# Two gate rows from rounded part and remainder, and eight modulation sums moved

## The reference, cut to what matters

```
mod = silu(c) @ w_ada + b_ada                       # 6 x 2048 values, the same for all tokens
sh1, sc1, g1, sh2, sc2, g2 = split(mod, 6)
h = rms_norm(x, norm1_w) * (1 + sc1) + sh1
... projections of h, two attentions, merged ...
x = x + g1 * (merged @ w_out)
h2 = rms_norm(x, norm2_w) * (1 + sc2) + sh2
x = x + g2 * ((silu(h2 @ w_ffn_gate) * (h2 @ w_ffn_up)) @ w_ffn_down)
return rms_norm(x, final_w)
```

## Time and profile before

| | |
|---|---|
| median of three runs | 2207.69 us |
| the profiled execution, its span from the first to the last instruction | 2206.6 us |
| TensorE busy | 2185.9 us (99%) |
| VectorE busy | 1492.7 us (68%) |
| ScalarE busy | 1013.1 us (46%) |
| GpSimd busy | 266.0 us (12%) |
| moved from HBM | 500.72 MB, 227 GB/s over the span |
| modulation sums on VectorE | 384 |
| loads of `ada_raw`, median to landing | 4.7 us |

### The profile page before, as it was taken

The page is one execution under the profiler, slowest core; times in us unless marked ns, Lnnn a source line. Parts: engine busy times, 40 slices in busy tenths (PEclk is TensorE's granted clock), DMA queues, the critical chain, the costliest instruction groups (busy, mean ns, idle before and its releaser), DMA issues.

```text
span 2206.6 us, 32483 instructions
## 1 busy us (share of the span) xinstructions
PE 2185.9 (99%) x10910; PEld 1849.9 (84%) x10910; DVE 1492.7 (68%) x1995; ACT 1013.1 (46%) x1246; POOL 266.0 (12%) x499
## 2 busy tenths in 40 slices
PE   9999999999999999999999999999999999999998
PEld 8898889988878887898888888888888888888886
DVE  5766668877777878587776768775566655444544
ACT  5445545444444445444555444454444444443433
POOL 2101110112210010701111211110000100000000
PEclk9999999999999999999999999999999999999999
DMA  8867576778986594968666877756776776565564
GB/s 294 246 194 233 177 271 232 194 247 292 304 282 182 164 313 141 262 201 263 220 193 198 294 262 244 250 199 225 237 233 218 255 239 210 176 224 181 186 200 138
DMA packets 200428, 500.72 MB, mean 227 GB/s; under 512 B 31816, under 2 KB 59112, under 8 KB 200048
## 3 DMA queue, kind: packets, MB, share of 16 engines
q1 hardware_dynamic: 166256, 394.10, 55.4%
q0 software_dynamic: 33760, 104.41, 14.9%
q10 hardware_dynamic: 288, 0.52, 0.1%
HBM read 496.84 MB, written 2.15 MB: 226 GB/s over the span
## 4 chain that ended last, share of the span: by engine, by line
PE 90%; DMA 4%; DVE 3%; ACT 1%; issue 1%; POOLq 0%; DVEq 0%; SPq 0%; ACTq 0%
PE ps L2251 73%; PE ps L2295 10%; DMA ada_raw<-in_w_ada_dram 2%; DMA raw<-in_ml_w_in_dram 1%; DVE lo L1225 1%; PE ps L2348 1%; PE ps L2719 1%; PE ps L2708 1%; DVE acc_s L1237 0%; PE ps L2609 0%; PE ps L2791 0%; DVE acc_g L1237 0%; PE ps L2443 0%; PE ps L2444 0%; PE ps L2466 0%
## 5 line engine op out<-in xcount | busy, mean ns | idle before, releaser
L1225 DVE TENSOR_TENSOR lo<-raw,hi 128x1024 fp32r<-128x1024 f32 x731 | 889.7, 1223 | 550.1 <-ACT hi L667 547.6
L667 ACT CAST hi<-raw 128x1024 fp32r<-128x1024 f32 x731 | 763.7, 1052 | 964.4 <-PE ps L2251 742.7
L2251 PE MATMUL ps<-hi,XH 128*128 128x512 f32 x1944 | 609.3, 393 | 3.6 <-DVE lo L1225 1.4
L2251 PE MATMUL ps<-lo,XH 128*128 128x512 f32 x1944 | 602.6, 390 | 0.0
L2251 PE MATMUL ps<-hi,XL 128*128 128x512 f32 x1944 | 602.0, 390 | 0.0
L2251 PEld LDWEIGHTS ps<-hi,XL 128*128 128x128 f32 x1944 | 365.0, 188 | 76.7
L2251 PEld LDWEIGHTS ps<-lo,XH 128*128 128x128 f32 x1944 | 365.0, 188 | 76.5
L2251 PEld LDWEIGHTS ps<-hi,XH 128*128 128x128 f32 x1944 | 360.8, 188 | 78.2 <-issue 4.1
L585 POOL DMA_DIRECT2D ada_raw<-in_w_ada_dram x384 | 206.5, 539 | 1552.2 <-DVE acc_s L1237 895.2
L1237 DVE SCALAR_TENSOR_TENSOR acc_s<-ada_raw,c_act,acc_s 128x512 f32<-128x512 f32 x256 | 191.1, 747 | 20.9 <-DMA ada_raw<-in_w_ada_dram 19.6
L2295 PE MATMUL ps<-XH,hi 128*128 (+1 forms) x504 | 142.9, 284 | 0.0
(11 more groups left out here) (385 smaller groups left out, 1833.1 us busy)
## 6 DMA issues: line engine op xcount, KB each, us to landing
ada_raw<-in_w_ada_dram POOLq DMA_DIRECT2D x384, 256.0 KB, 4.7
raw<-in_w_in_dram SPq DMA_DIRECT2D x136, 512.0 KB, 4.4
raw<-in_ml_w_in_dram SPq DMA_DIRECT2D x128, 512.0 KB, 4.7
raw<-in_w_gate_dram SPq DMA_DIRECT2D x176, 256.0 KB, 2.9
raw<-in_w_up_dram SPq DMA_DIRECT2D x176, 256.0 KB, 3.7
raw<-in_w_down_dram SPq DMA_DIRECT2D x88, 512.0 KB, 4.0
raw<-in_mla_w_in_dram SPq DMA_DIRECT2D x47, 512.0 KB, 4.9
raw<-in_mla_w_out_dram SPq DMA_DIRECT2D x32, 512.0 KB, 4.5
```

Of the source, the lines that this page charges most:

```text
L667: nc.scalar.copy(hi[:, j, :], raw[:, j, :]).then_inc(hi_ready, 1)
L1225: nc.vector.tensor_tensor(lo[:, j, :], raw[:, j, :], hi[:, j, :].bitcast(F32), ALU.subtract) \
L2251: ins = mm(ps[:, o:o + HALF], x, w[:, b % RING, c0:c0 + HALF], start=first, stop=(k == n_rows - 1 and x is xl), skip_group_check=True)
```

## The change

Gate rows: ScalarE rounds the sum `acc_g` into `gate1_hi` or `gate2_hi` (fp32r), in two halves; VectorE writes the remainder `gate_lo` over `acc_g` itself; TensorE adds both parts, with `ones` read as fp32r: eight fp32r matmuls of 128x512 per row in place of eight passes of f32. The roundings and subtractions stand after `kva` for `g1` and, for `g2`, in the second to last FFN pass behind its rounded product. `gate1_hi` lies where `g_row` will be written, `gate2_hi` where `g2_row` will be (over `ada_raw`, whose last sum is then used).

Sums: `z1` has 20 and not 16, `mv1` 17 and not 20, `mo_0` 17 and not 20, `mo_1` 18 and not 20, `mz0` and `mz1` 8 each and not 6. The total is the same, and the sums of `kv` to `mo1`, `mlk` and `mv0` are as many as before but four further on.

Further, the events `z0_half`, `mo1_half` and so on become one counter `first_half`, and `mo1_three` and `down1_three` one counter `three_quarters`; each wait asks for its place in the order in which they are raised.

```diff
-ADA_BESIDE = {"z1": 16, "kv": 12, "z0": 16, "mo0": 16, "mo1": 14, "mlq": 0, "mlk": 4, "mv0": 16, "mv1": 20, "mo_0": 20,
-              "mo_1": 20, "mz0": 6, "mz1": 6, "lo0": 8, "lo1": 10,
+ADA_BESIDE = {"z1": 20, "kv": 12, "z0": 16, "mo0": 16, "mo1": 14, "mlq": 0, "mlk": 4, "mv0": 16, "mv1": 17, "mo_0": 17,
+              "mo_1": 18, "mz0": 8, "mz1": 8, "lo0": 8, "lo1": 10,
...
+        gate1_hi = at("gate1_hi", 136, [P, D], F32R)
+        gate_lo = at("gate_lo", 104, [P, D], F32R)
...
+        gate2_hi = at("gate2_hi", 96, [P, D], F32R)
...
+        def half_of(name):
+
+            return ev("first_half"), HALVES.index(name) + 1
...
+            def gate_hi(dst, units):
+
+                act.wait_ge(ada_used, 16 * units)
+                for q in range(2):
+                    cols_ = slice(q * COLS, (q + 1) * COLS)
+                    nc.scalar.copy(dst[:, cols_], acc_g[:, cols_]).then_inc(ev("gate_hi"), 1)
...
             rest(B_KVA, 8)
+            gate_hi(gate1_hi, 12)
             first4(B_QB)
...
                 ffn_hi(p)
+                if p == FFN_PASSES - 2:
+                    gate_hi(gate2_hi, 24)
...
+            def gate_split(src, n):
+
+                for q in range(2):
+                    cols_ = slice(q * COLS, (q + 1) * COLS)
+                    dve.wait_ge(ev("gate_hi"), 2 * n - 1 + q)
+                    nc.vector.tensor_tensor(gate_lo[:, cols_], acc_g[:, cols_], src[:, cols_].bitcast(F32),
+                                            ALU.subtract).then_inc(ev("gate_lo"), 1)
...
             rest(B_KVA, 8, "kva")
+            gate_split(gate1_hi, 1)
             first4(B_QB)
...
                 ffn_lo(p)
+                if p == FFN_PASSES - 2:
+                    gate_split(gate2_hi, 2)
...
-            def ada_row(name, units):
+            def ada_row(name, src, count):
 
                 g = start(name)
-                pe.wait_ge(ada_used, 16 * units)
+                pe.wait_ge(ev("gate_lo"), count)
                 for n in range(4):
-                    ins = mm(ps[:, g + n * HALF:g + (n + 1) * HALF], ones[:, :], acc_g[:, n * HALF:(n + 1) * HALF],
-                             start=True, stop=True, skip_group_check=True)
+                    for part in (src, gate_lo):
+                        ins = mm(ps[:, g + n * HALF:g + (n + 1) * HALF], ones[:, :].bitcast(F32R),
+                                 part[:, n * HALF:(n + 1) * HALF], start=part is src, stop=part is gate_lo,
+                                 skip_group_check=True)
                 done(ins)
```

More of the change, by code:

```diff
@@ L352, in col, with three_of @@
             return pk[:, o:o + 1]
+        HALVES = ("z0", "mo1", "lo1", "ga0", "ga1", "ob1", "wo1", "down1")
+        THREES = ("mo1", "down1")
+        def half_of(name):
+            return ev("first_half"), HALVES.index(name) + 1
+        def three_of(name):
+            return ev("three_quarters"), THREES.index(name) + 1
         def complete(name):
@@ L861, in _ @@
                 if k == 7:
-                    act.wait_ge(ev("z0_half"), 1)
+                    act.wait_ge(*half_of("z0"))
                     nc.scalar.copy(z_tok[:, 0, 0:COLS], T("z0", 0)).then_inc(ev("z0_freed0"), 1)
@@ L1086, in gate_half @@
                 if tok == 0:
-                    act.wait_ge(ev(name + "_half"), 1)
+                    act.wait_ge(*half_of(name))
                     nc.scalar.copy(dst[:, 0, :], T(name, 0)).then_inc(ev(name + "_freed0"), 1)
@@ L1373, in last_residual @@
                 if tok == 0:
-                    dve.wait_ge(ev(name + "_half"), 1)
+                    dve.wait_ge(*half_of(name))
                 else:
@@ L1651, in quarter @@
                     mark(nc.vector.bn_stats(st[:, tok, 2 + cc, :], xs))
-            quarter("mo1", 0, (0, 1), (ev("mo1_half"), 1))
-            quarter("mo1", 1, (0,), (ev("mo1_three"), 1))
+            quarter("mo1", 0, (0, 1), half_of("mo1"))
+            quarter("mo1", 1, (0,), three_of("mo1"))
             def statistics(tok):
@@ L2100, in _ @@
                             split_merged("mTa", 0)
-                        dve.wait_ge(*(complete(name) if tok else (ev("ob1_half"), 1)))
+                        dve.wait_ge(*(complete(name) if tok else half_of("ob1")))
                     v = sig[q][:, tok, :]
@@ L2143, in _ @@
             rest(B_WO + 16, 16, "wo1")
-            dve.wait_ge(ev("wo1_half"), 1)
+            dve.wait_ge(*half_of("wo1"))
             gated_token("wo1", 1, 0, g_row, "x3")
@@ L2196, in _ @@
             rest(B_DOWN + KF, KF, g0=2)
-            dve.wait_ge(ev("down1_half"), 1)
+            dve.wait_ge(*half_of("down1"))
             gated_token("down1", 1, 0, g2_row, "x4")
@@ L2204, in last_quarter @@
             def last_quarter(c):
-                dve.wait_ge(*(complete("down1") if c else (ev("down1_three"), 1)))
+                dve.wait_ge(*(complete("down1") if c else three_of("down1")))
                 cols_ = slice(COLS + c * HALF, COLS + (c + 1) * HALF)
@@ L2281, in token_major @@
                         ins = token_part(g, nb, H, L, b, 0)
-                    ins.then_inc(ev(name + "_half"), 1)
+                    ins.then_inc(ev("first_half"), 1)
                     if half_done == "quarters":
@@ L2285, in token_major @@
                             ins = token_part(g, nb, H, L, b, 1, cs=(0,))
-                        ins.then_inc(ev(name + "_three"), 1)
+                        ins.then_inc(ev("three_quarters"), 1)
                     for b in range(b1 - RING, b1):
@@ L2500, in z_part @@
                 elif b == 15:
-                    ins.then_inc(ev("z0_half"), 1)
+                    ins.then_inc(ev("first_half"), 1)
             def out_part(b, tok):
@@ L2684, in vb_after @@
                 if b == 6:
-                    ada_row("g1", 12)
+                    ada_row("g1", gate1_hi, 2)
                 if b == 9:
@@ L2810, in down0_after @@
                 if b == 12:
-                    ada_row("g2", 24)
+                    ada_row("g2", gate2_hi, 4)
             token_major("down0", B_DOWN, KF, FH, FL, lambda k: (product_done, k // 4 + 1), then=down0_after)
```

## The result

After the change the kernel takes 2214.62 us (median of 7 runs, 2213.82 to 2215.52); before, measured beside it, 2207.69 (2206.63 to 2213.12). The ratio is 1.0026, interval [1.0016, 1.0035]: some 6.9 us lost, where 3.9 gained were forecast. The profiled execution took 2215.49 us with a span of 2213.8, 7.2 above that of before.

The account below looks back on a forecast made before the run. TensorE, busy 99% of the span and 90% of the chain, was taken to bound the kernel. Terms -3.2 + 0.4 - 2.9 + 1.8 + 0 = -3.9 us gave 2207.7 - 3.9 = 2203.8 us, range 2201.0 to 2207.2.

Parts of the forecast that it names:

- Order on GpSimd's queue: Sums four ahead from z1 to mv1 make unit 5 start in mlk; its loads still come in time, cost 0.
- D: Rival: z1 is pulled into the slow loads that follow, +2.4 us in all, 2210.1 us; chance 0.05.
- a wait that I did not see: Named, without place or size, as a way to be slower by more than 0.3%; chance of that outcome 0.03.
- Gate rows: Rows g1 and g2 on the chain: fp32r matmuls take 1.82 us each instead of 3.43, 3.2 us less.
- E: Rival: the gate rows don't get cheaper, fp32r keeping f32's pace; -0.7 us in all, 2207.0 us; chance 0.05.
- g1's preparation, mz0 and mz1: Roundings and subtractions after the last kva block, and two more sums each in mz0 and mz1: cost 0.
- g2's preparation: After pass 9's rounded product, new roundings and subtractions delay the next remainder: TensorE waits +0.4 us, bounds 0 and 0.8.
- Mixer projections: Eight sums leave mv1, mo_0 and mo_1, so waits there and at the first head shrink: -2.9 us, bounds 0 and 3.1.
- C: Rival: mixer projections stay short of data, only half of 2.9 us returns; 2205.3 us, 2206.8 with none; chance 0.17.
- z1's four sums: Four more sums in z1 make TensorE start qr near 101.6, not 99.93: +1.8 us, bounds 0 and 4.8.
- The walk: Stepping through VectorE's program in z1 with sum 0.7, subtraction 1.14, landing 5.3 us; it gave +1.8 us before qr.
- B: Rival: z1's sums stay hidden, -5.7 us in all, 2202.0 us, or 2201.6 without g2's stall; chance 0.28.

Follow-up runs that it names:

- the table alone: The kernel before with only the new dealing of the sums, gate rows still in f32: 2216.97 us, ratio 1.0039.
- the last experiment: Changed kernel with 14 sums in mv0, 19 in mv1, second gate's parts after block 15, 10 unread matmuls for 9 at the start: 2202.93 us, ratio 0.9973.
- the gate rows alone: The changed kernel with the sums dealt as before, so only the gate rows are new: 2206.5 us, ratio 0.9989.
- the 20, 14 and 19 sums: The changed kernel with z1 kept at 20 sums, mv0 at 14 for 16 and mv1 at 19 for 17: 2202.4 us, ratio 0.9968.

## Why the prediction was wrong

The step that failed is "Order on GpSimd's queue", with its "Cost 0". It saw the right kind of danger, that sums four ahead are wanted before GpSimd may load them, and checked it at one of the queue's waits, the one for the rows of X ahead of unit 5. There it was right: the memset came at 405.95, 403.7 without the start's 2.2, and nothing waited. The next one, for the gate logits ahead of unit 6, stands a few lines below and was left out; four sums ahead crossed it as well. In its place the runs showed a wait of 8.6 us and 2.0 us of lower pace behind it. By the prediction's own figures it could have been had: 78 sums before `mlq`, 4 in `mlk` and 16 in `mv0` are 98, and unit 6 begins at 96. The trace of before holds the times for it, too, in the lines shown above: the next loads after the wait are issued at 503.07, behind the small ones, and take about 4 us to land, while `mv0` ends near 504. No range or rival held this; D, the rival of the slower side, put its price in z1, and "a wait that I did not see" had no size. The range ended at 2207.2.

The other terms, each against the profile after:

- **Gate rows, -3.2**: right. 1.81 us each instead of 3.43, twice. E falls.
- **g1's preparation, mz0 and mz1, 0**: right. From the first head to `qb`, which holds all three, both chains take 280.2 us (652.69 to 932.93, 642.72 to 922.95).
- **g2's preparation, +0.4**: right place and mechanism, 0.6 us. The last feed-forward pass after, which answers to the earlier trace rows:
```profile
1934.14 2.01 ACT L759 CAST gate_hi<-acc_g 128x1024 fp32r<-128x1024 f32 x2
...
1935.42 2.35 DVE L1898 TENSOR_TENSOR gate_lo<-acc_g,gate_hi 128x1024 fp32r<-128x1024 f32 x2
...
1937.69 4.62 DVE L1249 TENSOR_TENSOR lo<-raw,hi 128x1024 fp32r<-128x1024 f32 x4
...
1938.96 0.73 PE L2286 MATMUL ps<-hi,XH 128*128 128x512 f32 x2 [0.31 <-DVE lo L1249]
```
The two subtractions stand between the pass's own remainder and the next block's.
- **Mixer projections, -2.9**: right, so far as it can be seen beside the new wait. Behind that one no wait for a remainder is left in `mv1`, `mo_0` and `mo_1`, and the first head waits 0.3 us instead of 1.50:
```profile
650.89 0.29 PE L2614 MATMUL ps<-ident,gi 8*128 8x8 f32 x2 [0.31 <-ACT oz L718]
```
From `mv0` to the heads: 8.6 + 2.0 - 2.9 = +7.7; the chain says +7.6. C falls.
- **z1's four sums, +1.8**: mis-sized. 0.1 us in this execution and 0.5 on average over the eight kernels, 1.8 being the largest. The walk's path is the one on the chain here: block 14's subtraction, the load of `w_qb`'s third block that it releases, that block's rounding and subtraction, then `CL`. The subtraction ended at 93.54, 91.3 without the start's 2.2, beside the walk's 91.6. (The 88.54 that the walk sets against its 91.6 is the start of block 15's subtraction; block 14's ends at 87.96 before.) The load behind it was too long in the walk: over 6.4 us, from 91.6 to "after 98", where the chain after has
```profile
93.57 5.27 DMA raw<-in_mla_w_qb_dram
```
So the block was split and `qr` began 1.6 us ahead of the walk. The sums' own transfers weren't it: their median was 5.0 us here and 5.2 to 5.6 in the seven others, beside the walk's 5.3. B was nearer in size, but its reason, that the sums stay hidden, holds in one profile only, the table alone, where `qr` waited for TensorE's own work; in the other seven VectorE's work in z1 stands on the chain ahead of `qr`. The Trainium skill's page "DMA: Bandwidth & Descriptors", section "Anatomy of one DMA — SWDGE (gpsimd) path", gives by its formula an estimate of 2.6 us for a load of one sum; measured are 5.0, so B came nearer for another reason than that rule. D falls: TensorE has no wait for a remainder in z1 after. With six more sums the ring of loads does stall z1 (26 sums, above), which a ring paced by that rule would not.
- **The start, +2.2**: in no term, and as far as the profiles tell not the change's (see the last experiment).

The sum over the profiled pair: -3.2 + 0.6 + 7.6 + 0.1 + 2.2 = +7.3, measured +7.2. Without the boundary the change is worth -3.2 + 0.6 - 2.9 + 0.5 = -5.0 by these terms, -4.9 and -5.6 by the spans of the two such kernels with the usual start and the second gate's parts in their first place (2201.7 and 2201.0 against 2206.6), and -6 to -7 by the ratios of the medians (0.9973 to 0.9968). The last 1 to 2 us are not accounted for. The kernel before has runs from 2205 to 2213 us, the ones without the boundary only 2201.5 to 2204.8, so its waits in the mixer projections may be longer in other executions than the profiled one shows (TensorE's waits for remainders are 1.4 us in it and 3.1 in the profile of the gate rows alone, with the same table). That was not tested.

## What to carry to other kernels

When work is dealt to earlier stages, count it up to every wait on the queue that feeds it, not only the first: list for each wait how many items are issued ahead of it and how many the consumer will have asked for by then, before and after. This boundary cost all or nothing: one item of 384 past it cost 11 us. And price a stall of TensorE with what follows it: here the products behind 8.6 to 9.1 us of idle took 1.4 to 2.0 us more.

## What the runs showed of the hardware

- After 8.6 us of idle TensorE's granted clock was at the lower level, and its first ten 512-column matmuls started 0.44 us apart; with the same stretch filled to the last 1.8 us by unread matmuls it was at the upper one throughout, and 2.1 us came back.
- The length of one gap alone does not decide it: with 26 sums in z1 the clock fell behind waits of 0.56 and 1.40 us close together, while the full pace was kept behind the 1.76 us after the fillers. It fell only when TensorE had gone on: the pairs at 95.31 and 95.88 came at the usual pace, or nearly (0.57 and 0.46 us), and those from 96.34 on at half.
- Unread 128-column f32 matmuls (two instructions each) took 0.23 us at the upper level (7.75 / 34) and 0.47 at the start of the program (4.21 / 9), where the column of the granted clock reads 1.00.
- 256 KB issued by GpSimd took a median of 5.0 to 5.6 us to land in z1 in the eight kernels with 20 sums there (longest 5.8 to 7.3) and 4.9 with 26 (longest 6.5), while the core moved 268 to 287 GB/s in all (60 to 98 us in the profiles of after, of the 20, 14 and 19 sums, and of 26).
